# A triangular inverse inside a matmul stream: 32x32 diagonal blocks on GpSimd and two merge levels on TensorE, in place of 16x16 blocks and three levels

## The reference, cut to what matters

```python
def step(S, inp):
    r_t, w_t, k_t, v_t, a_t, b_t = inp
    sa = jnp.einsum('bhij,bhj->bhi', S, a_t)
    S = S * w_t[:, :, None, :] + sa[..., None] * b_t[:, :, None, :] + v_t[..., None] * k_t[:, :, None, :]
    return S, jnp.einsum('bhij,bhj->bhi', S, r_t)
```

## Time and profile before

| | us |
|---|---|
| median of 3 runs | 3116.32 (3116.28 to 3119.73) |
| span of the profiled execution | 3114.6 |
| TensorE busy | 3019.7 |
| VectorE busy | 1697.0 |
| ScalarE busy | 1213.4 |
| GpSimd busy | 283.4 |

### The profile page before, as it was taken

How to read it: one execution, slowest core, us unless ns; L and a number is a source line. 1 busy time by engine, 2 the same in 40 slices (tenths; PEclk the granted TensorE clock), 3 DMA queues, 4 the chain that set the end, 5 groups by cost and what they waited for, 6 DMA issues and landing times.

```text
span 3114.6 us, 39362 instructions
## 1 busy us (share of the span) xinstructions
PE 3019.7 (97%) x15418; PEld 2423.6 (78%) x15418; DVE 1697.0 (54%) x2880; ACT 1213.4 (39%) x2131; POOL 283.4 (9%) x517
## 2 busy tenths in 40 slices
PE   9999999999999999999999999999999999999897
PEld 7778787878788877777778868787787887868786
DVE  6554545454543336556553364656666666565647
ACT  5443434343433324434343333434444343434422
POOL 0110101010100000000000002202022020212001
PEclk9999999999999999999999999999999999999999
DMA  4222222222243321221233322212222131224334
GB/s 164 82 77 84 78 82 82 82 82 82 82 135 131 106 88 62 68 75 62 68 122 134 122 85 80 83 55 90 75 70 90 61 97 56 89 72 140 135 129 155
DMA packets 86007, 288.99 MB, mean 93 GB/s; under 512 B 12080, under 2 KB 12720, under 8 KB 85568
## 3 DMA queue, kind: packets, MB, share of 16 engines
q1 hardware_dynamic: 69696, 243.66, 23.9%
q0 software_dynamic: 16128, 42.81, 4.5%
HBM read 261.13 MB, written 25.17 MB: 92 GB/s over the span
## 4 chain that ended last, share of the span: by engine, by line
PE 83%; DVE 9%; ACT 4%; issue 2%; DMA 1%; POOL 1%; DVEq 0%; ACTq 0%; SPq 0%; POOLq 0%
PE bank L280 14%; PE bank L282 14%; PE bank L281 14%; PE bank L284 7%; PE bank L286 7%; PE bank L285 7%; PE bank L1370 2%; PE bank L1301 1%; PE bank L1306 1%; DVE mc_split L736 1%; PE bank L337 1%; PE bank L317 1%; ACT mc_split L568 1%; PE bank L472 1%; PE bank L485 1%
## 5 line engine op out<-in xcount | busy, mean ns | idle before, releaser
L280 PE MATMUL bank<-ma_split,mc_split 128*128 128x512 f32 x2304 | 957.1, 415 | 12.7 <-DVE ma_split L890 7.7
L736 DVE TENSOR_TENSOR mc_split<-mc,mc_split 128x1024 fp32r<-128x1024 f32 x434 | 534.9, 1233 | 790.1 <-ACT mc_split L568 789.0
L282 PE MATMUL bank<-ma_split,mc_split 128*128 128x512 f32 x2304 | 905.8, 393 | 0.0
L281 PE MATMUL bank<-ma_split,mc_split 128*128 128x512 f32 x2304 | 902.4, 392 | 0.0
L568 ACT ACTIVATE mc_split<-mc 128x1024 fp32r<-128x1024 f32 x434 | 457.8, 1056 | 658.5 <-PE bank L284 349.6
L280 PEld LDWEIGHTS bank<-ma_split,mc_split 128*128 128x128 f32 x2304 | 436.8, 190 | 121.5 <-issue 49.1
L282 PEld LDWEIGHTS bank<-ma_split,mc_split 128*128 128x128 f32 x2304 | 434.6, 189 | 97.0
L281 PEld LDWEIGHTS bank<-ma_split,mc_split 128*128 128x128 f32 x2304 | 436.9, 190 | 78.7 <-issue 4.4
L284 PE MATMUL bank<-mc_split,ma_split 128*128 128x512 f32 x576 | 230.2, 400 | 5.0 <-DVE mb L1780 3.4
L286 PE MATMUL bank<-mc_split,ma_split 128*128 128x512 f32 x576 | 225.3, 391 | 0.0
L285 PE MATMUL bank<-mc_split,ma_split 128*128 128x512 f32 x576 | 224.7, 390 | 0.0
(11 more groups left out here) (366 smaller groups left out, 3732.6 us busy)
## 6 DMA issues: line engine op xcount, KB each, us to landing
mc<-in_w SPq DMA_DIRECT2D x434, 512.0 KB, 3.5
x<-mc POOLq DMA_DIRECT2D x8, 1024.0 KB, 5.2
y<-mb_split SPq DMA_DIRECT2D x28, 256.0 KB, 2.5
ma_split<-y POOLq DMA_DIRECT2D x28, 256.0 KB, 4.5
mb<-in_xt SPq DMA_DIRECT2D x8, 512.0 KB, 9.5
mc<-in_x POOLq DMA_DIRECT2D x4, 1024.0 KB, 5.7
mc<-x POOLq DMA_DIRECT2D x4, 1024.0 KB, 6.5
mats<-mc POOLq DMA_DIRECT2D x32, 128.0 KB, 2.2
```

The lines of the kernel that those rows point to most:

```text
L280: mm = pe.matmul(banks[j][:], wh[:, c], act_hi[:, kt, :], start=(kt == 0), stop=False)
L281: pe.matmul(banks[j][:], wl[:, c], act_hi[:, kt, :], start=False, stop=False)
L282: last = pe.matmul(banks[j][:], wh[:, c], act_lo[:, kt, :], start=False, stop=(kt == KT - 1))
L736: dve.tensor_tensor(w_low[:, s % NR, :, :], w_raw[:, s % NR, :, :], w_high[:, s % NH, :, :].bitcast(F32), ALU.subtract).then_inc(w_lo, 1)
```

## The change

`SUB` becomes 32 and the first level 5. Thus a matrix has 4 diagonal blocks and a unit 32 of them. GpSimd holds each block on four partitions: partition 32 r + b has the rows j of block b with j mod 4 = r, eight rows (`ROWS`) of 32. So `yb` and `yt` are 8x32 on 128 partitions, and the 31 steps k have two instructions each. All four groups of partitions need the whole block of A, which is loaded four times, now into the memory of `xw`. The identities come from a table `eye`, loaded once to `y0` and copied for each unit. The store of the inverses is four DMAs, one for each group. Level 4 is gone on TensorE, ACT and DVE; the six steps left stand at `begin + 62 + 5 (i - 4) // 2`, which is 62, 64, 67, 69, 72 and 74, where levels 4 to 6 stood at 54, 56, 59, 61, 64, 66, 69, 71 and 74. The rest of the chunk part keeps its points.

```diff
-SUB = 16
+SUB = 32
-FIRST_LEVEL = 4
+FIRST_LEVEL = 5
+ROWS = 2 * NCH * SUBS * SUB // P
...
-            ub, yb, yt = [rc_(SUB, SUB)[0:2 * NCH * SUBS] for _ in range(3)]
+            y0, yb, yt = [rc_(ROWS, SUB) for _ in range(3)]
+            ub = xw.rearrange("p q n -> p (q n)").rearrange("p (j i) -> p j i", i=SUB)
...
-                if i < 13:
-                    return begin + 54 + 5 * (i - 4) // 2
+                if i < STATE:
+                    return begin + 62 + 5 * (i - 4) // 2
...
-                pool.dma_start(ub, blocks(a["mats"])).then_inc(ub_in, 16)
+                groups = [slice(2 * NCH * SUBS * r, 2 * NCH * SUBS * (r + 1)) for r in range(SUB // ROWS)]
+                for rows in groups:
+                    pool.dma_start(ub[rows, 0:SUB - 1, :], blocks(a["mats"])[:, 0:SUB - 1, :]).then_inc(ub_in, 16)
...
-                pool.memset(yb, 0.0).then_inc(inv_step, 1)
-                pool.wait_ge(inv_step, n + 1)
-                pool.memset(yb.rearrange("p j i -> p (j i)")[:, 0:SUB * SUB:SUB + 1], 1.0).then_inc(inv_step, 1)
-                pool.wait_ge(ub_in, 16 * (u + 1))
+                pool.tensor_copy(yb, y0).then_inc(inv_step, 1)
+                pool.wait_ge(ub_in, 16 * len(groups) * (u + 1))
                 for k in range(SUB - 1):
-                    size = [2 * NCH * SUBS, k + 1, SUB - 1 - k]
+                    kept = k // len(groups) + 1
+                    size = [P, kept, SUB - 1 - k]
...
-                pool.dma_start(blocks(a["inv"]), yb).then_inc(yb_out, 16)
-                pool.wait_ge(yb_out, 16 * (u + 1))
+                for r, rows in enumerate(groups):
+                    pool.dma_start(blocks(a["inv"])[:, r::len(groups), :], yb[rows, :, :]).then_inc(yb_out, 16)
+                pool.wait_ge(yb_out, 16 * len(groups) * (u + 1))
...
+                pool.wait_ge(x1_turned, 2 * KT)
+                pool.wait_ge(x1_sq, 2 * KT)
+                pool.dma_start(y0, a["eye"]).then_inc(eye_in, 16)
```

More of the change, by code:

```diff
@@ L1103, in programs @@
                                                      sem("xt_in"))
-            held = sem("held")
+            held, eye_in = sem("held"), sem("eye_in")
             o_var, o_root, o_ready = sem("o_var"), sem("o_root"), sem("o_ready")
@@ L1118, in programs @@
             LANE0 = RW0 + 2
-            CHUNK_K = 24
+            STATE = 4 + 3 * (LEVELS - FIRST_LEVEL)
+            CHUNK_K = STATE + 3 * NCH - 1
             PART_B, CHUNKS = 8, 12
@@ L1284, in chunk_pe @@
                                 mm.then_inc(c_pe, 1)
-                elif i < 13:
+                elif i < STATE:
                     lv, part = FIRST_LEVEL + (i - 4) // 3, (i - 4) % 3
@@ L1307, in chunk_pe @@
                         mm.then_inc(c_pe, 1)
-                    if i == 11:
+                    if i == STATE - 2:
                         chunk_r(pe, u, 0)
                 elif i % 3 == 1:
-                    c = (i - 13) // 3
+                    c = (i - STATE) // 3
                     c_wait(pe, "dve", u, f"T{LEVELS - 1}{c // 2}")
@@ L1338, in chunk_pe @@
                 else:
-                    c = (i - 12) // 3
+                    c = (i - STATE + 1) // 3
                     c_wait(pe, "dve", u, f"S{c - 1}")
@@ L1491, in chunk_act @@
             def chunk_act(act, u, i):
-                if 4 <= i < 13 and (i - 4) % 3 < 2:
+                if 4 <= i < STATE and (i - 4) % 3 < 2:
                     lv, part = FIRST_LEVEL + (i - 4) // 3, (i - 4) % 3
@@ L1500, in chunk_act @@
                         act.activation(to, frm, ACT.Copy).then_inc(c_act, 1)
-                if i == 11 or i >= 15 and i % 3 == 0:
-                    c = 0 if i == 11 else (i - 12) // 3
+                if i == STATE - 2 or i >= STATE + 2 and i % 3 == 0:
+                    c = 0 if i == STATE - 2 else (i - STATE + 1) // 3
                     c_wait(act, "pe", u, f"R{c}")
                     act.activation(r0s, C_BANK[f"R{c}"][:, 0:P], ACT.Copy).then_inc(c_act, 1)
-                if i >= 13 and i % 3 == 2:
-                    c = (i - 13) // 3
+                if i >= STATE and i % 3 == 2:
+                    c = (i - STATE) // 3
                     c_wait(act, "pe", u, f"O{c}")
@@ L1999, in sub_inverses @@
-                pool.memset(yb, 0.0).then_inc(inv_step, 1)
-                pool.wait_ge(inv_step, n + 1)
-                pool.memset(yb.rearrange("p j i -> p (j i)")[:, 0:SUB * SUB:SUB + 1], 1.0).then_inc(inv_step, 1)
-                pool.wait_ge(ub_in, 16 * (u + 1))
-                for k in range(SUB - 1):
-                    size = [2 * NCH * SUBS, k + 1, SUB - 1 - k]
+                    pool.wait_ge(yb_out, 16 * len(groups) * u)
+                else:
+                    pool.wait_ge(eye_in, 16)
@@ new lines, in sub_inverses @@
+                n = (2 * SUB - 1) * u
+                pool.tensor_copy(yb, y0).then_inc(inv_step, 1)
+                pool.wait_ge(ub_in, 16 * len(groups) * (u + 1))
+                for k in range(SUB - 1):
+                    kept = k // len(groups) + 1
+                    size = [P, kept, SUB - 1 - k]
+                    pool.wait_ge(inv_step, n + 2 * k + 1)
+                    pool.tensor_tensor(yt[:, 0:kept, k + 1:SUB], yb[:, 0:kept, k:k + 1].broadcast_to(size),
+                                       ub[:, k:k + 1, k + 1:SUB].broadcast_to(size), ALU.mult).then_inc(inv_step, 1)
@@ L2005, in sub_inverses @@
                     pool.wait_ge(inv_step, n + 2 * k + 2)
[L2006 to L2009, removed]
+                    pool.tensor_tensor(yb[:, 0:kept, k + 1:SUB], yb[:, 0:kept, k + 1:SUB], yt[:, 0:kept, k + 1:SUB],
@@ L2159 @@
     ang = (np.arange(SEQ, dtype=np.float32)[:, None] * inv[None, :]).astype(np.float64)
+    eye = np.eye(SUB, dtype=np.float32).reshape(ROWS, SUB // ROWS, 1, SUB).transpose(1, 2, 0, 3).repeat(2 * NCH * SUBS, axis=1
+                                                                                                        ).reshape(P, ROWS, SUB)
     bones = np.kron(np.eye(2), np.ones((HD, HD))).astype(np.float32)
@@ L2173 @@
         "sin": np.sin(ang).astype(np.float32).reshape(TT, P, ROT).transpose(1, 0, 2),
-        "bones": bones,
+        "bones": bones, "eye": eye,
         "reset": np.tile((np.arange(SEQ) % CH != 0).astype(np.float32)[None], (P, 1)),
```

6 lines of the change are left out of this document (2 added, 4 removed).

## The result

The changed kernel takes 3176.85 us (median of 4 runs, 3172.39 to 3179.99), before 3116.3. The ratio is 1.019, with a 95% interval of 1.0175 to 1.0201: slower by 60 us. The forecast was 3172 us, and the sign, the size and the place of the loss were as forecast. That it came so close is in part luck: the term for the waits on GpSimd was 11 us too large, the term for the clock 16 us too small, and waits that it counted at nothing grew by 5 us.

The account below looks back on a forecast made before the run. TensorE, 97% busy with products in program order, was taken as the bound. Level 4 -35.5, stalls +80.8 and clock +10.2 gave +55.5 us: profiled 3114.6 becomes 3170.1, predicted median 3172 us, range 3112 to 3225 (8 in 10).

Parts of the forecast that it names:

- the term for the waits on GpSimd: TensorE's stalls before level 5, per unit chain growth plus 3.5 us less the room: 80.8 us in sum.
- the term for the clock: TensorE at half speed for 3.4 us after each of six stalls over 3.5 us, 1.7 us each: 10.2 us.
- Level 4 out of the stream: TensorE loses 8 transposes and two groups of 8 products per unit: 4.4 us a unit, 35.5 us saved in eight.
- The chain, A = 22.4 us: Growth per unit of GpSimd's chain, from arithmetic, loads and stores: 22.4 us, from 9.6 to 31.
- the arithmetic: GpSimd's inversion, 62 instructions instead of 30, interference included: 32.6 us a unit, 17.2 us more.
- The loads: Loading diagonal blocks by four DMAs of 992 128 B pieces instead of one: taken as 8 us, +4.
- The stores: Storing the inverses by four DMAs of 256 pieces instead of 1024 pieces: +1.2 us, ends +0.7 and +2.1.
- the first rival: GpSimd's time not in proportion, interference fading, DMAs overlapping: 3102 us with growth of 12, 3087 at the floor; 14%.
- the second rival: Small pieces make the loads slow or serialised, 15.6 us in a row: chain growth 31, +127.7, 3244 us; 8%.
- the floor of the load: Lower end for loading the blocks: last issue 2.5 us after the first, plus 3.3 us, 5.8 us.
- together level 5 begins 3.5 us sooner: TensorE reaches level 5 4.4 us sooner without level 4, less 0.9 us for its place one point later.
- The third rival: Stalls let VectorE catch up, so TensorE's later waits for it shrink; counted at nothing, no chance given.

Follow-up runs that it names:

- `te_only`: Changed kernel with GpSimd still inverting 16x16 blocks as before, so only TensorE's part of the change (merge from 16 to 32 left out): 3085.25 us, ratio 0.990.
- `shift5`: Changed kernel with the merge and state steps of units 1 to 7 five points later, unit 0 as it is: 3145.46 us.
- `squares_shift5`: Changed kernel with diagonal squares stored contiguously and loaded by one DMA, and merge and state steps of units 1 to 7 five points later: 3131.37 us, ratio 1.0035.
- `gp_only`: Changed kernel with TensorE doing all three levels at their old points, so only GpSimd's part of the change: 3270.67 us.

## Why the prediction was right, and where its terms were off

**Level 4 out of the stream, -35.5 us.** Right. `te_only` gives it back, and with -35.5 all nine sums close within 3.1 us.

**The chain, A = 22.4 us.** Measured as the time from the load of the blocks to the load of `xt`, after less before: 24.2, 22.1, 23.9, 19.5, 21.5, 19.9, 22.4 and 22.4 us, mean 22.0. Of its parts, the arithmetic (+17.2 forecast) took 32.4 us and 15.7 before: +16.7. The loads (+4) took 9.1 and 4.1: +5.0. The stores (+1.2) took 4.4 and 4.0: +0.4, as the small stores land in 2.0 us. The assumption that decides it was that interference stays in proportion over the longer run; it did, and the first rival fell with it. The choice of 8 us for the load, near the rows of small pieces rather than those of large ones, was 1 us too low, and the second rival (15.6) was far off. Two small slips of the working touch only the lower end: the floor of the load was added up with 3.3 us where the row has 3.9, and 62 quiet instructions at 0.75 us a pair are 23.3 us, not 22.5. The figure of the Trainium skill's DMA: Bandwidth & Descriptors (section Anatomy of one DMA), by which the load should be no longer than before, was not followed by the trace: 6.0 us from issue to landing of each DMA, 9.1 until the data could be used.

**The stalls, 80.8 us.** By unit the forecast was 15.5, 2.2, 10.3, 11.0, 11.8, 14.8, 14.8 and 0.4; the trace has 17.6, 0.6, 8.6, 9.0, 10.0, 9.5, 16.1 and 0, in sum 71.6. The order of the units was right but for unit 5. Of the 9 us between the sums, 3 are the chains: with each unit's own growth in place of A the formula gives 77.6. The other 6 lie in the step "together level 5 begins 3.5 us sooner". From the first load of the blocks to the place where TensorE begins to wait, the changed kernel is 3.9, 2.2, 0.5, 4.5, 2.6, 0.8 and 4.8 us shorter in units 0 to 6. It is near level 4's 4.4 in units 0, 3 and 6. In units 2, 4 and 5 a wait for VectorE's masked copies (L1226) in the hg lane now lies in that stretch, of 2.67, 1.24 and 2.10 us, and in unit 5 another 4 us at a clock of 0.57 (in unit 1 a slow stretch shown below takes 1.5 us more than in the kernel before). While TensorE stands or runs slowly there, GpSimd's chain goes on, and the later stall is shorter by that time. The waits of units 2 and 5:

```profile
2183.42 0.82 PE L1373 MATMUL bank<-mb 128*128 128x128 f32 x5 [2.67 <-DVE mb L1226]
...
2590.66 0.55 PE L1373 MATMUL bank<-mb 128*128 128x64 f32 x3 [2.10 <-DVE mb L1226]
```

**The clock, 10.2 us.** This term was mis-sized: 1.7 us for each of six stalls, and nothing elsewhere. The changed kernel lost 26.1 us more than the one before. The slow stretch after the six stalls lasted 3.7 to 6.1 us instead of 3.4, which is 15.5 us instead of 10.2 (2.9, 1.9, 2.9, 2.8, 2.0 and 3.0). The row of before that it was sized by, after a stall of 3.5 us, is at the short end. The other 10.6 us lie elsewhere, nearly all of them after waits for other things, of 1.4 to 7.4 us, where the slow stretch is now longer or new. This is the stretch of the kernel before from 2026 on, and the one that answers to it in the changed kernel from 2042.5 on:

```profile
2026.00:2030.00 4.00, 3.24 (x12) 2.98 (x13) 2.83 (x5) 0.00 (x0) 0.00 (x0) 0.57 0.00 0
...
2042.50:2049.50 7.00, 5.97 (x18) 5.10 (x19) 4.64 (x7) 0.63 (x1) 5.90 (x15) 0.51 0.00 0
```

That the change causes these 10.6 us is not shown. The profiled execution of `te_only` has 10.5 of them without an added stall, and its other three executions, with the clock of the kernel before, do not seem to have them. And the length of a slow stretch differs between executions where nothing else does. At 1845 us, in a part in which the changed kernel and `shift5` are the same program, TensorE waits 4.3 us in both; then come, in the changed kernel and in `shift5`:

```profile
1845.50:1851.50 6.00, 5.92 (x13) 3.99 (x14) 3.99 (x7) 0.61 (x2) 0.00 (x0) 0.50 0.29 87
...
1845.50:1851.50 6.00, 5.54 (x16) 3.58 (x17) 4.25 (x7) 0.92 (x2) 0.00 (x0) 0.72 0.27 87
```

The one runs at half clock throughout, the other for a little over half of it. After the wait of 2.67 us at 2183 the first profile of the changed kernel shows full clock, the second one, after the same wait of 2.70, 0.57 for 4 us. The two profiles agree in the sum all the same (45.3 and 45.5), and all eight executions of the changed kernel have a mean granted clock of 0.974 to 0.978. What sets the length of a stretch is open.

**Other waits.** The prediction counted them at nothing and expected that they would, if anything, shrink, because VectorE catches up in the stalls. They grew by 4.6 us in the changed kernel (74.6 idle more, 70.0 of it on `inv`), and by another 9 in the kernels that start five points later (`shift5`, `squares_shift5`). The third rival was wrong in sign. The growth is in TensorE's waits for VectorE's masked copies in the hg lane, and it comes with the level that is gone, not with the stalls: 4.5 us in the kernel before, 7.9 in `te_only`, which has no stall, 8.9 in the changed kernel, and 4.2 in `gp_only`, which keeps level 4 and has the longest stalls. Before, and in `te_only`:

```profile
PE bank L1370 <- DVE mb L1223: 4.5, 4, 2.7
...
PE bank L1371 <- DVE mb L1224: 7.9, 6, 2.7
```

The sum was +55.5 and the spans differ by 63.4: the waits on `inv` 11 too high (80.8 for a change of 70.0), the clock 16 too low, the other waits 5 too low, and 2 us by which the account itself does not close.

## What to carry to other kernels

Before moving work from the busiest engine to an idle one, follow the idle engine's chain to the point where the busy engine needs it, and compare its growth with the room there, unit by unit; an engine that is 9% busy can still be the one that is late. For small dependent instructions count instructions, not elements. A later start only helps by what the stream does in between: here the wait stands 8 points later than before, but the merge level that left the stream had lain there with 4.4 us a unit, and TensorE comes to the transposes of level 5 sooner than before, not later.

## What was not expected of the hardware

A stall costs more than its length. After stalls of 8.6 to 17.6 us TensorE ran at half clock for another 3.7 to 6.1 us, worth 2 to 3 us each; after shorter waits elsewhere, of 1.4 to 7.4 us, it did so for up to 7 us or not at all, and not always for the same time in two executions of the same program. Filling most of a stall with useless products made the kernel at least 7 us faster. GpSimd's small dependent instructions took 0.29 us on average while VectorE ran nothing, and 0.51 while it worked. Small stores to DRAM of 32 KB landed in 2.0 us; four issued in a row took 4.4 us until the next load could be issued, where one of 64 KB in 64 B pieces, which lands in 3.2 us, took 4.0.
